# Two coarse levels of a chunked recurrence computed as blocks inside the diagonal product's plane

## The reference, cut to what matters

```python
# S_t = diag(f_t) S_{t-1} + k_t outer v_t (k_t = 1 - f_t), o_t = S_t^T q_t
b = jnp.cumsum(fb, axis=2)
diff = b[:, :, :, None, :] - b[:, :, None, :, :]
decay = jnp.where(causal, jnp.exp(jnp.where(causal, diff, 0.0)), 0.0)
scores = jnp.einsum('bhtc,bhsc,bhtsc->bhts', qb, kb, decay)
o = jnp.einsum('bhts,bhsv->bhtv', scores, vb) + jnp.einsum('bhtc,bhcv->bhtv', qb * jnp.exp(b), s)
```

## Time and profile before

| | us |
|---|---|
| median of 3 runs | 2658.11 (2656.72 to 2660.35) |
| the profiled execution's own time | 2658.96 |
| its span | 2657.2 |
| PE busy | 2447.8 (92%) |
| PE weight loads busy | 2199.4 (83%) |
| DVE busy | 1904.1 (72%) |
| ACT busy | 1372.5 (52%) |
| POOL busy | 1322.1 (50%) |

### The profile page before, as it was taken

How to read it: one execution, slowest core, us unless ns; L and a number is a source line. 1 busy time by engine, 2 the same in 40 slices (tenths; PEclk the granted TensorE clock), 3 DMA queues, 4 the chain that set the end, 5 groups by cost and what they waited for, 6 DMA issues and landing times. The chain is left out here.

```text
span 2657.2 us, 40710 instructions
## 1 busy us (share of the span) xinstructions
PE 2447.8 (92%) x15142; PEld 2199.4 (83%) x15142; DVE 1904.1 (72%) x3031; ACT 1372.5 (52%) x2032; POOL 1322.1 (50%) x1313
## 2 busy tenths in 40 slices
PE   4999999999999999999986999699999999999990
PEld 4889898898998989989875765599999999999980
DVE  7475765757758567585686787588888888888875
ACT  3433625436245262452633322377777777777772
POOL 6354664646546556465564364344544544544330
PEclk9999999999999999999987999799999999999995
DMA  5201111111111111101113323489999999999995
GB/s 183 60 26 33 54 34 46 33 40 45 42 45 34 41 38 41 53 25 41 45 73 121 103 73 130 145 259 297 295 307 304 290 309 304 298 304 308 353 329 169
DMA packets 207424, 380.80 MB, mean 143 GB/s; under 512 B 22586, under 2 KB 129402, under 8 KB 206714
## 3 DMA queue, kind: packets, MB, share of 16 engines
q1 hardware_dynamic: 180330, 302.31, 33.0%
q0 software_dynamic: 25664, 71.41, 11.9%
q10 hardware_dynamic: 1232, 4.46, 0.4%
HBM read 313.79 MB, written 72.97 MB: 146 GB/s over the span
## 5 line engine op out<-in xcount | busy, mean ns | idle before, releaser
L121 PE MATMUL ps<-xTh,w_mix_low 128*128 128x368 f32 (+1 forms) x1728 | 595.1, 344 | 10.2 <-POOL w_mix_low L115 8.8
L122 PE MATMUL ps<-xTl,w_mix_high 128*128 128x368 f32 (+1 forms) x1728 | 568.9, 329 | 0.0
L123 PE MATMUL ps<-xTh,w_mix_high 128*128 128x368 f32 (+1 forms) x1728 | 566.4, 328 | 0.0
L2062 POOL DMA_INDIRECT ys_d<-yo,tab_early x114 | 215.3, 1888 | 453.9 <-DVE yo L2222 312.8
L121 PEld LDWEIGHTS ps<-xTh,w_mix_low 128*128 128x128 f32 x1728 | 325.7, 188 | 21.8 <-issue 18.6
L122 PEld LDWEIGHTS ps<-xTl,w_mix_high 128*128 128x128 f32 x1728 | 325.8, 189 | 9.1 <-issue 6.3
L123 PEld LDWEIGHTS ps<-xTh,w_mix_high 128*128 128x128 f32 x1728 | 325.3, 188 | 0.0
L2103 PE MATMUL ps<-xghl,wgh 128*128 128x320 f32 (+5 forms) x1024 | 268.2, 346 | 10.4 <-DVE xghl L115 5.9
L2103 PE MATMUL ps<-xghl,wuh 128*128 128x320 f32 (+5 forms) x1024 | 263.4, 344 | 0.0
L2105 PE MATMUL ps<-xghl,wgl 128*128 128x160 f32 (+5 forms) x1024 | 240.6, 235 | 0.0
L2105 PE MATMUL ps<-xghl,wul 128*128 128x160 f32 (+5 forms) x1024 | 238.3, 233 | 0.0
(11 more groups left out here) (369 smaller groups left out, 5945.9 us busy)
## 6 DMA issues: line engine op xcount, KB each, us to landing
wd_early<-in_w_exp_down SPq DMA_DIRECT2D x64, 1024.0 KB, 8.8
wg_early<-in_w_exp_gate SPq DMA_DIRECT2D x124, 512.0 KB, 7.8
wu_early<-in_w_exp_up SPq DMA_DIRECT2D x124, 512.0 KB, 5.4
w_mix_raw<-in_w_in SPq DMA_DIRECT2D x72, 512.0 KB, 3.9
mT_d<-gs_m SPq DMA_DIRECT2D x8, 544.0 KB, 2.7
xr_m<-in_x_prompt SPq DMA_DIRECT2D x8, 512.0 KB, 3.8
xn_d<-xr_m SPq DMA_DIRECT2D x8, 512.0 KB, 2.9
out<-vrow_m SPq DMA_DIRECT2D x8, 512.0 KB, 4.8
```

Of the source, the lines that this page charges most:

```text
L121: pe.matmul(out, ll, rh, start=start, stop=False)
L122: pe.matmul(out, lh, rl, start=False, stop=False)
L123: return pe.matmul(out, lh, rh, start=False, stop=stop)
L2062: pool.indirect_dma_start(out=ys_d[:, :], out_offset=rows_of(e, j, m), in_=yo[:m, b, j, :], in_offset=None, compute_op=ALU.add, bounds_che ...
```

## The change

The planes of levels 32 and 64 are gone. `FULL` is 5, the number of levels below 32. Those five still have one full matmul and a plane each. For levels 32 and 64 `products` runs one matmul for each block that the level has: two of 32 x 32 outputs (s in rows 0 to 31 with t in 32 to 63, s in 64 to 95 with t in 96 to 127) and one of 64 x 64 (s in 0 to 63, t in 64 to 127). They are written into plane 0, over the diagonal product's values, which aren't wanted there. In the chunk of 64 rows it is one of 32 x 32. Mask 0 now keeps the diagonal and all blocks of 32 above it. DVE's product and sum run over 6 planes in all chunks. The selects of levels 5 and 6 are gone, and the mask of plane 0 is made by one select and one addition of the identity. `diffs`, `exps` and `times` are as before.

```diff
+FULL = sum(hw < 32 for hw in LEVELS)
...
-            masks = c2.enter_context(nc.sbuf_tensor("masks", [P, NL + 1, P], F32))
+            masks = c2.enter_context(nc.sbuf_tensor("masks", [P, FULL + 1, P], F32))
...
-        x, pm = sb("x_m", [P, 2, NL + 1, 256]), sb("pm_m", [P, 2, NL + 1, P])
+        x, pm = sb("x_m", [P, 2, NL + 1, 256]), sb("pm_m", [P, 2, FULL + 1, P])
...
-            CONSTANTS = 3 + 3 * NL + 2
+            CONSTANTS = 3 + 3 * FULL + 2
...
                         for i in SLOT_LEVELS[cn // 2]:
-                            xs = x[:, slot, i, xo:xo + m]
-                            if 2 * LEVELS[i] <= m:
+                            xs, hw = x[:, slot, i, xo:xo + m], LEVELS[i]
+                            if i < FULL:
                                 mm = pe.matmul(ps[:m, PB[(i + 1) // 4], (i + 1) % 4 * P:(i + 1) % 4 * P + m], xs, xs,
                                                start=True, stop=True)
+                                continue
+                            for lo in range(0, m - hw, 2 * hw):
+                                hi = lo + hw
+                                mm = pe.matmul(ps[lo:hi, PB[0], hi:hi + hw], xs[:, lo:hi], xs[:, hi:hi + hw], start=True, stop=True)
                         mm.then_inc(p_done, 1)
...
-                        s = NL + 1 if m == P else NL
+                        s = FULL + 1
...
-                    if 1 <= t < 8:
+                    if 1 <= t <= FULL:
                         level(t - 1)
-                keep(masks[:, 0, :], 0, [[1, P]], -1)
-                keep(masks[:, 0, :], 0, [[-1, P]], 1)
+                keep(masks[:, 0, :].rearrange("p (g u) -> p g u", u=32), -1, [[32, P // 32], [0, 32]], -1)
+                pool.tensor_tensor(masks[:, 0, :], masks[:, 0, :], ident[:, :], ALU.add).then_inc(built, 1)
+                n += 1
```

## The result

The changed kernel takes 2667.49 us (median of 10 runs, 2662.63 to 2669.94), the kernel before in the same 10 rounds 2658.82. The ratio is 1.0028, 95% interval 1.0020 to 1.0036: slower by 7.4 us (5.3 to 9.6) by the ratio, by 8.7 us by the medians. The forecast was +10.4 us.

What follows compares the result with a forecast made beforehand. PE was taken to bound the kernel. Full chunks 13.0, first chunks -1.8, short chunks 0.4 and the last head's end -1.2 gave +10.4 us: 2669.4 for the profiled execution, predicted median 2668.5, range 2658 to 2680.

Steps and rivals of the forecast that it cites:

- What bounds the kernel: Mid-mixer: PE's work sets the time; DVE's counts only in each head's first wait and at the last head's end.
- The waits of the earlier trace: PE's waits for POOL and DVE's z, 2.5 us a head, might swallow delay: about 2659.4, in a rival of chance 0.20.
- The price of a change of form: PE in a full chunk: switching column form drains the engine, 0.12 to 0.14 us an end; three changes about 0.44 us.
- if that were all: PE in a full chunk: counting only the columns saved, the change would save 0.21 us.
- the rival at 2640.4: Block matmuls run without a drain, PE saves 0.207 us a full chunk, together -17.7 us; chance 0.12.
- The chunk's sum: Full chunks on PE: 0.24 us more each, over 55 chunks +13.0 us (5.5 to 25.3).
- the other two at 0.29 and 0.32: Full chunk on PE: start times of the last two 32-column passes, in us from level 16's last pass.
- the bound of 0.058: Upper bound in us for a 32-column pass on PE, as if passes had a floor; 0.031 was taken.
- First chunk of a head: Wait for the mask product: product 0.275 us shorter, `p_done` 0.05 later, 8 x -0.22 = -1.8 us.
- Short chunk: Level 32's two passes get a mode of their own: +0.06 us each in 7 heads, +0.4 us.
- Last head's end: DVE runs almost without a gap there and loses 1.65 us of work; taken as -1.2 us (-1.65 to 0).
- Entry: POOL loses six selects but waits 6.37 us for PE, so costed at nothing; without that cover 3.1 us.

Runs made afterwards that it cites:

- experiment 1: Changed kernel with DVE's product and sum over 8 planes again (7 in the short chunk), unused planes masked to zero: 2672.07 us, ratio to before 1.0048.
- experiment 2: Changed kernel with the blocks' order 32, 64, 32 columns, so four changes of form a full chunk instead of three: 2678.74 us, ratio to before 1.0066.
- experiment 6: Changed kernel with only level 64 as a block, level 32 a full matmul with its own plane (7 planes on DVE): 2670.66 us, ratio to before 1.0045.
- experiment 3: Changed kernel with the 64 x 64 block split into two of 32 stationary and 64 moving columns: 2658.67 us, ratio to before 0.9996.
- experiment 5: Changed kernel with all products in 56 small 32-column passes a chunk, ordered by column group: 2652.18 us, ratio to before 0.9972.

## Why the prediction was right, point by point

**What bounds the kernel.** Right. 47 us more on DVE moved the time by 3 to 5 us (experiment 1), 0.17 us more a chunk on PE moved it by 11 (experiment 2). The waits of the earlier trace rows that I had thought might absorb a part absorbed nothing.

**The price of a change of form.** Right as a mechanism, and shown from both sides: one more costs 11.2 us and one less gives 8.8 back, both with a part that is blocks running side by side, and experiment 6 has 0.15 us a change without that part. In the changed kernel's timeline the first block starts 0.20 us after the last full pass, as read off (0.107 + 0.095). The Trainium skill's rule in "TensorEngine Tiling (Array Packing)", Key Properties, that a change of mode drains the engine and a change of tile within a mode doesn't, agrees with this for all three forms (0.12 to 0.15 us a change; in experiment 3 passes of 32 and of 64 moving columns in one form follow without such a gap). What it would have been "if that were all" (0.21 us a chunk saved, the rival at 2640.4) didn't occur.

**The chunk's sum.** The term is too large: I had +0.237 us a full chunk. L654's first pass to L123 shows +0.15, and the way from the second chunk's start to the ninth's is 67.0 to 67.1 us for 65.8 or 65.9 in the first seven heads, about +0.17 to +0.19 a chunk; why single chunks lie between +0.03 and +0.31 there stays open. The step that is off is "the other two at 0.29 and 0.32", the two 32-column blocks one behind the other. They lie in different column groups and ran side by side, all four passes within 0.06 us (their starts are in experiment 2). So from the last full pass to the transpose it takes 0.65 us, not 0.70, and L123 follows 0.34 later, not 0.37. With 0.18 a chunk the term is 55 x 0.18 = 9.9 us for 13.0. The sentence of the Trainium skill on parallel tiles (same page and section) had this, with up to 3.4 us as an estimate, and I had left it beside the sum; the trace agrees with it. The pass of 32 columns, which no row showed, costs 0.032 us in one group (experiment 5), as the line through two sizes gave it (0.031); the bound of 0.058 was far off.

**First chunk of a head.** Foretold -0.22 us each; the interval to the second chunk is 2.99 us for 3.26 in all eight heads, -0.27. The wait is 0.79, foretold near 0.8. The term is -2.2 for -1.8.

**Short chunk.** +0.06 us, foretold +0.06.

**Last head's end.** Foretold -1.2, too much. The last head is 0.83 us shorter than in experiment 1, which has DVE's old work. Of that 0.27 is the first chunk's wait, counted above, so -0.6 can be shown for the end. The stretches at half clock differ between the traces there, so it isn't sharper than that.

**Entry.** Foretold nothing. The +1.6 us of the profiled execution appear where the clock dips, as the window shows. Ahead of it PE's starts differ by 0.35 us at most, and by less than 0.1 at 60 us, so POOL's shorter list shows no cost there. One profile of each can't tell whether it makes the dip likelier.

**The new sum** is 9.9 - 2.2 + 0.4 - 0.6 = +7.5 us. The ratio says 7.4 (5.3 to 9.6), the medians 8.7, and the two traces, from head 0's first product to the output projection without the 0.9 us at half clock, 6.9. The forecast of +10.4 was 2 to 3 us too high, because the chunk's term was 3 us too large and the saving at the end, too large as well, took back 0.6.

## What to carry to other kernels

Here matmuls with 32 or 64 stationary columns between full ones paid 0.12 to 0.15 us each on entry and on exit, and that was more than the columns they saved until many of them stood together. Count the changes of form in a stretch before counting columns. If the stretch can stay in the narrow form, put neighbouring passes in different column groups: here 56 small passes took 0.69 us for the 1.87 of 12 full and 6 small ones, and the kernel became 2.3% faster, where the half-way version was 0.3% slower than doing nothing.

## What the runs showed that I had not expected

- Passes with 32 stationary and 32 moving columns in four different column groups follow each other after 0.008 us, or about 0.010 with the blocks and the change of form counted in; in one group after 0.032. I had expected 0.014 and 0.031.
- A dip of the granted clock to half for 3.4 us in the entry, behind the same wait of 1.35 us, came in the changed kernel's profile and not in the one before. It costs 1.6 us, a fifth of the effect under study, and would have been booked on the change if only the two spans had been compared. Profiles of the same entry code differ by up to 2.6 us there.
- The first six heads of one trace repeat closely: 169.30 to 169.42 us a head before, 170.12 to 170.59 in the changed kernel. So a difference of 1 us a head can be read from one profile each, while two medians of ten runs leave 4 us of interval.
